# Two chained transformer blocks on one core: pairing the latent-attention values, regrouping the router, and reordering VectorE in the neighbourhood-attention loop

## The reference, cut to what matters

```python
y_na = neighborhood_attention(q, k, v, kc, vc, rpb)   # 16 heads of 32, one softmax over window + context
# hyena_mixer: for each of two orders
y = irfft(rfft(u, n=2 * L) * K, n=2 * L)[:L] + u * skip   # long_conv
y = x1 * y                                                # and x2 in the second order
```

```python
logits = h @ w_router + b_router                 # 256 x 8
top_val, top_idx = lax.top_k(logits, 2)
top_w = jax.nn.softmax(top_val, axis=-1)
```

## Time and profile before

| | us |
|---|---|
| median of 3 runs | 2389.74 |
| lowest and highest | 2387.16, 2394.24 |
| time of the profiled execution | 2388.43 |
| its span in the profile | 2387.1 |
| PE busy | 2295.7 (96%) |
| DVE busy | 1800.2 (75%) |
| ACT busy | 1226.5 (51%) |
| POOL busy | 411.0 (17%) |

### The profile page before, as it was taken

The page is one execution under the profiler, slowest core; times in us unless marked ns, Lnnn a source line. Parts: engine busy times, 40 slices in busy tenths (PEclk is TensorE's granted clock), DMA queues, the critical chain, the costliest instruction groups (busy, mean ns, idle before and its releaser), DMA issues.

```text
span 2387.1 us, 27392 instructions
## 1 busy us (share of the span) xinstructions
PE 2295.7 (96%) x10949; PEld 1734.8 (73%) x10949; DVE 1800.2 (75%) x2024; ACT 1226.5 (51%) x1436; POOL 411.0 (17%) x447
## 2 busy tenths in 40 slices
PE   6988999999999999899999899999999999999998
PEld 2455897545599877447996588788887888788886
DVE  4756787687698855675664388989888888889897
ACT  1243653223255321334433377777767676767775
POOL 1234570134165010452220000000000000000000
PEclk9999999999999999999999999999999999999999
DMA  8633568541647874134664379989998999899995
GB/s 328 251 156 106 229 256 314 221 192 72 220 177 282 322 304 185 53 142 176 247 247 172 115 290 361 353 333 358 355 361 327 361 356 355 328 369 352 366 352 216
DMA packets 49463, 630.36 MB, mean 264 GB/s; under 512 B 7456, under 2 KB 8049, under 8 KB 11633
## 3 DMA queue, kind: packets, MB, share of 16 engines
q1 hardware_dynamic: 44192, 618.81, 68.6%
q10 hardware_dynamic: 2752, 6.99, 0.8%
q0 software_dynamic: 2384, 2.73, 0.3%
HBM read 624.83 MB, written 3.67 MB: 263 GB/s over the span
## 4 chain that ended last, share of the span: by engine, by line
PE 82%; DVE 10%; ACT 3%; issue 2%; DMA 2%; POOL 1%; ACTq 0%; SPq 0%; DVEq 0%
PE psum L1198 19%; PE psum L1199 19%; PE psum L1200 19%; PE psum L1064 5%; PE psum L1093 4%; PE psum L2655 3%; DVE sbuf L727 2%; DVE ring_r L1193 2%; PE psum L2658 1%; PE psum L3276 1%; DVE sbuf L1340 1%; DMA ring<-in_t_ada 1%; PE psum L2316 1%; PE psum L3176 1%; DMA ring<-in_t_mlp 1%
## 5 line engine op out<-in xcount | busy, mean ns | idle before, releaser
L1199 PE MATMUL psum<-ring_r,sc_r 128*128 128x512 f32 x1688 | 665.1, 394 | 0.0
L1193 DVE TENSOR_TENSOR ring_r<-ring,sbuf_r 128x2048 fp32r<-128x2048 f32 (+1 forms) x287 | 536.7, 1876 | 141.2 <-ACT sbuf_r L1184 139.7
L1184 ACT CAST sbuf_r<-ring 128x2048 fp32r<-128x2048 f32 (+1 forms) x287 | 445.6, 1556 | 313.3 <-PE psum L1200 255.9
L1193 DVE TENSOR_TENSOR ring_r<-ring,sc_r 128x2048 fp32r<-128x2048 f32 (+1 forms) x243 | 476.2, 1969 | 107.3 <-ACT sc_r L1184 106.5
L1184 ACT CAST sc_r<-ring 128x2048 fp32r<-128x2048 f32 (+1 forms) x243 | 398.3, 1643 | 246.6 <-PE psum L1200 224.2
L1198 PE MATMUL psum<-sbuf_r,sc_r 128*128 128x512 f32 (+1 forms) x1148 | 425.6, 371 | 3.5 <-DVE ring_r L1193 3.1
L1199 PEld LDWEIGHTS psum<-ring_r,sc_r 128*128 128x128 f32 x1688 | 316.9, 188 | 72.0 <-issue 1.4
L727 DVE SCALAR_TENSOR_TENSOR sbuf<-ring,sbuf 128x512 f32<-128x512 f32 x405 | 332.7, 828 | 15.0 <-DMA ring<-in_t_ada 9.5
L1200 PE MATMUL psum<-sbuf_r,sc_r 128*128 128x512 f32 x860 | 339.6, 395 | 0.0
L1198 PE MATMUL psum<-sc_r 128*128 128x512 f32 x828 | 331.1, 400 | 0.0
L1200 PE MATMUL psum<-sc_r 128*128 128x512 f32 x828 | 324.3, 392 | 0.0
(11 more groups left out here) (367 smaller groups left out, 2749.8 us busy)
## 6 DMA issues: line engine op xcount, KB each, us to landing
ring<-in_t_moe SPq DMA_DIRECT2D x168, 2048.0 KB, 7.8
ring<-in_t_ada SPq DMA_DIRECT2D x48, 2048.0 KB, 9.0
ring<-in_t_mlp SPq DMA_DIRECT2D x32, 2048.0 KB, 8.1
ring<-in_t_win SPq DMA_DIRECT2D x17, 2048.0 KB, 9.0
ring<-in_t_ffn SPq DMA_DIRECT2D x16, 2048.0 KB, 8.1
ring<-in_t_out SPq DMA_DIRECT2D x7, 2048.0 KB, 8.8
ring<-in_t_bias SPq DMA_DIRECT2D x2, 2048.0 KB, 8.3
spectra<-sc POOLq DMA_DIRECT2D x5, 512.0 KB, 4.2
```

Source lines behind the costliest of these rows:

```text
L1184: p.act.e.copy(p.r(hi), src).then_inc(*p.sig("high", st.tag, n))
L1193: p.dve.e.tensor_tensor(p.r(src), src, p.r(hi), ALU.subtract).then_inc(*p.sig("lowp", st.tag, n))
L1199: e.matmul(out, l[0], r[1], start=False, stop=False)
```

## The change

In layer 0's loop the values of two heads are multiplied together, their matmuls taking turns, and there are four `PT` buffers. In layer 2's loop the reciprocal of job i moves from round i to round i + 1, behind that round's maximum (and behind its copies); DVE's part of a convolution step is cut in two, the first in the same round as before, the second behind the reciprocal of the next round; POOL's part moves to the next round, behind that round's scaling. The router's 8 matmuls are spread over four groups of 32 rows, weights padded from 8 to 32 columns, and a matmul with a selecting matrix adds the groups; six fillers are placed on PE; the rest of the rows (L3146) is computed by POOL instead of DVE.

```diff
         self.mla = mla = Heads("mla", [sc[:, 13824 + 256 * i:14080 + 256 * i] for i in range(4)],
-                               [xn[:, 512 * i:512 * i + 512] for i in range(2)], [(i,) for i in range(4)], [(4,), (5,)], 3,
-                               dil.DG)
+                               [xn[:, 512 * i:512 * i + 512] for i in range(4)], [(i,) for i in range(4)], [(4,), (5,)], 3,
+                               dil.DG, pair=True)
...
-def dve_conv(p, m):
+def dve_conv(p, m, part):
...
+        if part == 0:
+            p.dve.wait_ge(*p.at("freq", o, c))
...
+            e.tensor_tensor(p.YF[c], p.bank[6], kh(c), ALU.mult)
+            e.tensor_tensor(TM[:, 0, :], p.bank[7], kh(2 + c), ALU.mult).then_inc(*p.sig("real", o, c))
+        else:
+            e.tensor_tensor(p.YF[2 + c], p.bank[6], kh(2 + c), ALU.mult)
+            e.tensor_tensor(TM[:, 1, :], p.bank[7], kh(4) if c == 0 else kh(1), ALU.mult).then_inc(*p.sig("spectra", o, c))
...
     dve_max(p, p.na, 0)
-    dve_over(p, p.na, 0)
     for i, one, two, end in steps(p.na):
-        dve_round(p, p.na, one if i else None, two, end)
+        dve_round(p, p.na, one if i else None, two, end, i - 1)
         if i % 4 == 3 and i < 32:
-            dve_conv(p, i // 4)
+            dve_conv(p, i // 4, 0)
+        if i % 4 == 0 and 0 < i <= 32:
+            dve_conv(p, i // 4 - 1, 1)
...
         if one is not None:
             pool_scale(p, p.na, one)
-        if i % 4 == 3 and i < 32:
-            pool_conv(p, i // 4)
+        if i % 4 == 0 and 0 < i <= 32:
+            pool_conv(p, i // 4 - 1)
...
-        ins = e.matmul(p.bank[2][0:8, 0:256], p.RW[:, k, :], p.HT[:, k, :], start=(k == 0), stop=(k == 7))
+        g = 32 * (k % 4)
+        ins = e.matmul(p.bank[2][g:g + 32, 0:256], p.RW[:, k, :], p.HT[:, k, :], start=(k < 4), stop=(k >= 4))
     ins.then_inc(*p.sig("logits"))
+    pe_constants(p, 6, (256,))
+    p.pe.wait_ge(*p.at("select"))
     p.pe.wait_ge(*p.at("turnedlogits"))
     for b in range(2):
-        ins = e.transpose(p.bank[3][:, 8 * b:8 * b + 8], p.LT[:, 128 * b:128 * b + 128], p.IDENT[0:8, 0:8])
+        ins = e.matmul(p.bank[3][:, 8 * b:8 * b + 8], p.LT[:, 128 * b:128 * b + 128], p.SEL, start=True, stop=True)
     ins.then_inc(*p.sig("logitsT"))
+    pe_constants(p, 6, (512, 512, 256))
     p.pe.wait_ge(*p.at("chosen"))
...
+    pe_constants(p, 6, (512,))
...
-def dve_rows_parts(p):
+def pool_rows_parts(p):
...
     pool_added(p, 6)
+    pool_rows_parts(p)
```

More of the change, by code:

```diff
@@ L179, in lay @@
     return {"small": small, "gains": gains, "k_tri_iota": np.concatenate([tables_1["k_tri"], tables_1["k_iota"]], 1),
-            "router": np.ascontiguousarray(w.reshape(8, 128, 8).transpose(1, 0, 2).reshape(128, 64)),
+            "router": np.pad(w.reshape(8, 128, 8).transpose(1, 0, 2), ((0, 0), (0, 0), (0, 24))).reshape(128, 256),
             "k_feats": tables["k_feats"], "k_win": tables["k_win"], **lay_tiles(v)}
@@ L233 @@
     "dve_once": ("condcopy", "posf", "vecs", "maskb", "latents", "lamsum", "shorts", "subln", "filterset", "ctxn",
-                 "edges", "second", "chosen", "placed", "flag", "turnedlogits"),
+                 "edges", "second", "select", "chosen", "placed", "flag", "turnedlogits"),
     "act_once": ("silu", "latsq", "lamexp", "ctxsq", "secondexp", "keysA"),
@@ L503, in stages @@
         self.mla = mla = Heads("mla", [sc[:, 13824 + 256 * i:14080 + 256 * i] for i in range(4)],
-                               [xn[:, 512 * i:512 * i + 512] for i in range(2)], [(i,) for i in range(4)], [(4,), (5,)], 3,
-                               dil.DG)
+                               [xn[:, 512 * i:512 * i + 512] for i in range(4)], [(i,) for i in range(4)], [(4,), (5,)], 3,
+                               dil.DG, pair=True)
         for h in range(8):
-            mla.causal(self, h, h % 2, QT[0:96, h, :], KT[0:96, h, :])
-            mla.rows(h, 2, 64, [KV[:, k, 128 * h + 64:128 * h + 128] for k in range(2)], v3(mla.PT[h % 2], 2), [6, 7],
+            mla.causal(self, h, h % 4, QT[0:96, h, :], KT[0:96, h, :])
+            mla.rows(h, 2, 64, [KV[:, k, 128 * h + 64:128 * h + 128] for k in range(2)], v3(mla.PT[h % 4], 2), [6, 7],
                      HT[:, h // 2, :], False)
@@ L1316, in pe_pair_values @@
         for h in pair:
-            ins = p.pe.e.matmul(p.bank[h.bank][h.r0:h.r0 + h.v[kb].shape[1], 0:256], h.v[kb], h.pt[:, kb, :],
+            q0 = 0 if (h.both or kb % 2 == 0) else 128
+            ins = p.pe.e.matmul(p.bank[h.bank][h.r0:h.r0 + h.v[kb].shape[1], q0:256], h.v[kb], h.pt[:, kb, q0:256],
                                 start=(kb == 0), stop=(kb == n - 1))
@@ L2778, in dve_conv @@
         kh = lambda i: p.KH[:, i, 512 * o:512 * o + 512]
-        p.dve.wait_ge(*p.at("freq", o, c))
-        p.dve.wait_ge(*p.total("kh_in"))
-        if o and c == 0:
-            p.dve.wait_ge(*p.at("time", 0, 1))
-        if c:
-            p.dve.wait_ge(*p.at("product", o, 0))
-        e.tensor_tensor(p.YF[c], p.bank[6], kh(c), ALU.mult)
-        e.tensor_tensor(TM[:, 0, :], p.bank[7], kh(2 + c), ALU.mult).then_inc(*p.sig("real", o, c))
-        e.tensor_tensor(p.YF[2 + c], p.bank[6], kh(2 + c), ALU.mult)
@@ L2788, in dve_conv @@
-        e.tensor_tensor(TM[:, 1, :], p.bank[7], kh(4) if c == 0 else kh(1), ALU.mult).then_inc(*p.sig("spectra", o, c))
+        if part == 0:
+            p.dve.wait_ge(*p.at("freq", o, c))
+            p.dve.wait_ge(*p.total("kh_in"))
+            if o and c == 0:
+                p.dve.wait_ge(*p.at("time", 0, 1))
+            if c:
+                p.dve.wait_ge(*p.at("product", o, 0))
+            e.tensor_tensor(p.YF[c], p.bank[6], kh(c), ALU.mult)
[3 more added lines that the diff above has]
+            e.tensor_tensor(TM[:, 1, :], p.bank[7], kh(4) if c == 0 else kh(1), ALU.mult).then_inc(*p.sig("spectra", o, c))
@@ L2789, in dve_conv @@
     else:
         b = step - 2
-        if b == 0:
-            p.dve.wait_ge(*p.at("product", o, 1))
-        p.dve.wait_ge(*p.total("skip_in"))
-        if o and b == 0:
-            p.dve.wait_ge(*p.at("convolved", 0, 1))
-        p.dve.link(e.tensor_tensor(TM[:, b, :], HZ[:, b, 0:512], p.SKIP[o], ALU.mult))
-        p.dve.wait_ge(*p.at("time", o, b))
-        e.tensor_tensor(TM[:, b, :], TM[:, b, :], p.bank[6 + b], ALU.add).then_inc(*p.sig("skipped", o, b))
-        p.dve.wait_ge(*p.at("skipped", o, b))
@@ L2800, in dve_conv @@
-        e.tensor_tensor(HZ[:, b, 512 * o:512 * o + 512], TM[:, b, :], HZ[:, b, 512 * (o + 1):512 * (o + 2)],
-                        ALU.mult).then_inc(*p.sig("convolved", o, b))
+        if part == 0:
+            if b == 0:
+                p.dve.wait_ge(*p.at("product", o, 1))
+            p.dve.wait_ge(*p.total("skip_in"))
+            if o and b == 0:
+                p.dve.wait_ge(*p.at("convolved", 0, 1))
+            e.tensor_tensor(TM[:, b, :], HZ[:, b, 0:512], p.SKIP[o], ALU.mult).then_inc(*p.sig("skipped", o, b, 0))
+        else:
+            p.dve.wait_ge(*p.at("skipped", o, b, 0))
+            p.dve.wait_ge(*p.at("time", o, b))
+            e.tensor_tensor(TM[:, b, :], TM[:, b, :], p.bank[6 + b], ALU.add).then_inc(*p.sig("skipped", o, b, 1))
+            p.dve.wait_ge(*p.at("skipped", o, b, 1))
+            e.tensor_tensor(HZ[:, b, 512 * o:512 * o + 512], TM[:, b, :], HZ[:, b, 512 * (o + 1):512 * (o + 2)],
+                            ALU.mult).then_inc(*p.sig("convolved", o, b))
@@ L3169, in pe_pick @@
             ps = p.bank[2 + r]
-            p.pe.wait_ge(*p.at("rowlow", "n7", 1))
+            p.pe.wait_ge(*p.at("rowrest", "n7", 1))
             p.pe.wait_ge(*p.at(*held[2 + r]))
```

18 lines of the change are left out of this document (10 added, 8 removed).

## The result

The changed kernel took 2416.99 us as the median of four runs (2410.76 to 2418.91); the kernel before took 2388.99 beside it (2387.16 to 2394.24). The ratio is 1.0102, with a 95% interval of 1.0083 to 1.0121: slower by 20 to 29 us. The prediction was 2406.5 with a range of 2394 to 2415. Sign and mechanism came out as forecast. The size did not: the median lies 2 us above the top of the range, and the loss is 28 us against a forecast of 17. Four runs beside four don't place the size better than that: by the ratio the loss is 24.4 us, which on the 2389.7 of the forecast gives 2414.1. The kernel before, run 15 to 27 times later, has medians of 2392.5 to 2393.1. The four times go with the mean granted clock of their executions: 2410.76 at 0.986, the other three, 2416.83 to 2418.91, at 0.982.

What follows compares the result with a forecast made beforehand. No engine is full in layer 2's loop; a ring of waits across PE, DVE, ACT and POOL bounds it. 10.8 + 5.1 + 1 + 0 = +17 us on 2389.7 gives 2406.5, range 2394 to 2415.

Steps and rivals of the forecast that it cites:

- The ring: Layer 2's loop: the cycle of waits across PE, DVE, ACT and POOL between convolution steps gets longer, +10.8 us in all.
- Clock falls in the loop: Layer 2's loop: longer PE idle pieces drop its clock to 1.2 GHz more often, +5.1 us.
- 5.5 slow steps: Layer 2's loop: forecast count of convolution steps slowed by a clock fall, against 2 before.
- the two I held for certain, 2 and 6: Layer 2's loop: convolution steps counted as slow, with 2.4 and then 2.0 us of PE idleness ahead.
- the five that I judged by the length of their wait: Layer 2's loop: other convolution steps, their waits between one that fell and one that didn't; half counted as slow.
- a fall costs 1.46 us on the ring: Layer 2's loop: price per slow convolution step, 5.06 us at the low level against 3.60.
- My upper end of 8.8: Layer 2's loop: the clock term's top, +8.8 us, if all eight convolution steps are slow.
- Layer 0's loop, 0: Interleaved values win a few tenths inside and lose them at the end: 0 us, ends -1 and +1.7.
- Router, +1: Router: faster logits, but DVE's small operations held by POOL's subtractions: +1 us, ends -3.4 and +1.6.
- The hold: Router: POOL's two subtractions, 2.5 us each, block DVE's small operations from SBUF; that term is +1.2 us.
- Without the hold: Router: if POOL's subtractions don't block DVE's small operations, the earlier logits gain 1.8 us.
- The first gather at the low clock: Router: 3.80 us for 16 matmuls against 2.15 later; fillers could win 1.65, a third of it taken.

Runs made afterwards that it cites:

- run 15: Not a run's label: the words say the kernel before, unchanged, was run 15 to 27 times later, with medians of 2392.5 to 2393.1 us.
- run with fillers: The changed kernel plus constant multiplications on PE in the idle pieces of layer 2's loop; 2405.43 us, ratio 1.0054 to the kernel before.
- the version with the spectrum first: The changed kernel with PE fillers in layer 2's loop, none ahead of two backward steps, and POOL's spectrum operations ahead of its scaling; 2404.95 us.
- the version with late rows: The kernel before with the router's regrouped logits and fillers, both row subtractions late on DVE, gate arithmetic behind them; 2389.79 us, ratio 0.9984.
- the one with three fillers: The kernel before with layer 0's interleaved values and four PT buffers, plus 0.85 us PE fillers ahead of the last three latent transpositions; 2393.13 us.

## Why the prediction was right, and where it fell short

- **The ring, +10.8: right.** The turns at the high clock are the forecast ones within 0.12 us each (run with fillers). At the high clock the loop is 84.3 (85.29 less 1.0) against 73.63 before: +10.7. The reciprocals carry it: alone they make all four turns behind a forward step some 13.4 long. The split takes that down to 11.2 for two of them, and for the other two the spectrum behind the scaling is the last link, as the version with the spectrum first shows.
- **Clock falls in the loop, +5.1: right in number, too small in price.** I counted 5.5 slow steps and six came; the two I held for certain, 2 and 6, are the slowest (6.62 and 6.12), though their waits were 1.8 us twice and not 2.4 and 2.0. Among the five that I judged by the length of their wait the count is luck: behind 1.68 and 2.19 us the step was slow, behind 1.85 it wasn't, and behind 2.40 it was once and once not. The step that failed is "a fall costs 1.46 us on the ring". That was the one row of a step slowed over part of its length. The six steps are together 13.1 longer than six of 3.60, 2.2 each, and 5.69 to 6.62 appear where the clock stayed low for some 7 us. Taken over the loop, low clock now holds 11.7 us and the last step's 1.69, 13.4 in all, against 2.1 before (75.70 less 73.63): +11.3 instead of +5.1, or +9.1 against the longest profile of an unchanged loop (77.88). My upper end of 8.8 used the same price and was too low with it. (The ends of all terms add up to 2396 and 2413 and not to 2397 and 2412, which changes nothing.)
- **Layer 0's loop, 0: the mechanism right, the choice wrong.** The time won by interleaving is nil as said (25.10 against 25.35). The clock fall that I had only as the end of the range (+1.7) is there in all four profiles with the interleaved values and an unfilled tail. The part alone costs 2.6 us by its median; its ratio gives 0.5 to 6.7.
- **Router, +1: right.** +0.8 at the gather, +0.9 at the first expert matmul. The hold took 0.93 and 2.00 us at the two operations; the logits' gain of some 2 us was eaten by it. Without the hold I had -1.8, and the version with late rows gives -1.6. The page SBUF — State Buffer of the Trainium skill says in its rule on the shared port pair that a DVE operation with two SBUF inputs contends with a POOL operation that reads SBUF, and that one with at most one SBUF input, outside the 2-port modes, does not. The trace agrees here: L3116, with one input, took 0.17 while POOL was at work, and L3117 and L3120, with two, ended together with POOL's. The row that I took for an example, L840, was none of this kind: it has one tensor input. That it ended when POOL's operation did (1.26 us) made the hold likely, and no more. The fillers in the router are five, where the section on the change has six.
- **The first gather at the low clock:** it stayed slow (24 records in 4.84, the clock low from 1395.9 on for some 7 us). I had held that likely and counted a third of the 1.65 us; nothing of it came.
- **What is not explained by the change.** Ahead of layer 2's loop the changed kernel is 5.8 us late in its profile, more than layer 0's part. Low pieces near 129, 194, 260 and 600 to 635 us come and go from one profile to the next, and those near 173 and 577 differ in length, with nothing changed there. Over the profiles whose layer 0 is that of before and has no fillers the first convolution step starts between 979.3 and 982.3. So up to 3 us of that delay is of this kind. Layer 2's loop has it too: in the four profiles besides that of before whose loop is unchanged it is 75.71, 77.09, 77.44 and 77.88 long, so 18 to 20 of the 20.3 us are the change's. And so have the timed runs: among the 27 of the kernel before in the first group, the fastest (2386.20) had a mean granted clock of 0.992 and the slowest (2397.90) one of 0.987, and those between go with their clock too. Most of the spread of one kernel is low clock that comes and goes.

By medians the four parts alone cost 18.3, 3.5, -1.1 and 2.6 us against their common median of before (2392.5), together 23.3. The ratio of the whole change is worth 24.4 us of 2389. The totals add up within their intervals, but that is in part chance: in the profiles the loop is 21.3 us longer with the reciprocals alone and 5.7 with the split alone, and 20.3 with both.

## What to carry to other kernels

A reciprocal (or any small operation) that waits for another engine is only worth moving if what stands behind it is not also what the next stage waits for: follow the ring all the way round, and count everything that is put in front of it. The price of one more wait on TensorE is not its length alone: idle pieces near 2 us brought stretches of 3.5 to 7 us at 1.2 GHz that cost as much again as the longer ring (11.3 beside 10.7 us), and cheap constant matmuls in the idle pieces took that half back. A subtraction moved to POOL for relief should be placed where DVE has no operations with two SBUF inputs: two of 2.4 us on POOL made two of 0.17 us on DVE 2.6 us longer together.

## What the runs showed of the hardware

- The length of an idle piece does not decide on the clock by itself. The same wait of 2.21 to 2.23 us at the start of layer 0's latent loop was followed at once by a low piece in the changed kernel, in its version with fillers and in the router part alone, and by none in the kernel before, in layer 0's part alone and in the version with the spectrum first. Within the changed kernel 2.40 us ahead of 1029.20 was outlasted and 2.40 ahead of 1080.93 was not; nor was 1.68 ahead of 1040.22.
- Less work for PE can cost time: with overlapping matmuls in the tail of layer 0 a low piece of some 7 us stood there in four of four profiles, in none of seven without them and not in the one with three fillers; it cost 1.2 us of the stage.
- POOL's TENSOR_SCALAR does not hold DVE as its TENSOR_TENSOR does. It did so only near the start, for 0.4 to 0.5 us and not for the length of the other: DVE's L2801 (128x512, two SBUF inputs) took 1.17 us at 1014.38, 0.05 behind the start of POOL's scaling, and 0.67 at 1030.57, where it came first. L2807, of the same kind, began 0.52 us into a scaling of 1.56 (1025.05 beside 1024.53) and took the usual 0.70. And before, POOL's scaling took 1.95 at 1006.93, 0.17 behind the start of such a DVE operation (L2796), instead of 1.56.
